# The delta rule's block inverse with full-array transposes and products in place of 64-row ones

## The reference

```
low = where(strict, einsum('bhncd,bhnsd->bhncs', k * beta, k) * decay, 0)
T = triangular_solve(eye + low, eye)          # (I + low)^-1, lower triangular
u = T @ (v * beta);  w = T @ (k * beta * exp(G))
# scan over the chunks: v_new = u - w @ s;  o = (q exp(G)) @ s + qk @ v_new;  s = s * g_last + k_dec^T @ v_new
```

## Time and profile before

| | us |
|---|---|
| median of 3 runs | 1845.88 |
| lowest and highest | 1842.76, 1850.29 |
| profiled execution, its own time | 1848.1 |
| its span, first to last instruction | 1845.4 |
| TensorE busy | 1555.1 (84%) |
| VectorE, ScalarE, GpSimd busy | 826.0, 371.3, 193.0 |
| mean granted TensorE clock | 0.90 |

### The profile page before, as it was taken

The page is one execution under the profiler, slowest core; times in us unless marked ns, Lnnn a source line. Parts: engine busy times, 40 slices in busy tenths (PEclk is TensorE's granted clock), DMA queues, the critical chain, the costliest instruction groups (busy, mean ns, idle before and its releaser), DMA issues. The chain is left out here.

```text
span 1845.4 us, 19291 instructions
## 1 busy us (share of the span) xinstructions
PE 1555.1 (84%) x7431; PEld 933.9 (51%) x7431; DVE 826.0 (45%) x1536; ACT 371.3 (20%) x702; POOL 193.0 (10%) x282
## 2 busy tenths in 40 slices
PE   4999972689999799476799859999889799999877
PEld 2877662688444444242334325444564456646563
DVE  2344549344344377442112133355664325555553
ACT  3212153111101100110001010100450134622230
POOL 0000027300000000001000000000450001202330
PEclk8899976668999899678899979999899899999887
DMA  9221002210877476669999974252300221131101
GB/s 353 79 91 46 1 1 46 53 27 4 306 244 270 175 279 219 233 254 417 416 395 365 389 263 170 91 182 69 137 1 23 91 91 46 46 136 47 47 1 46
DMA packets 126745, 283.72 MB, mean 154 GB/s; under 512 B 28568, under 2 KB 30904, under 8 KB 121403
## 3 DMA queue, kind: packets, MB, share of 16 engines
q1 hardware_dynamic: 123056, 266.78, 39.5%
q0 software_dynamic: 3600, 15.73, 2.1%
HBM read 312.90 MB, written 4.19 MB: 172 GB/s over the span
## 5 line engine op out<-in xcount | busy, mean ns | idle before, releaser
L2245 PE MATMUL ps<-hT,ring 128*128 128x512 f32 x400 | 176.4, 600 | 0.3 <-issue 0.3
L1312 PE MATMUL ps<-ring,hTx 128*128 128x512 f32 x320 | 139.2, 593 | 1.9 <-PEq L178 1.8
L2245 PEld LDWEIGHTS ps<-hT,ring 128*128 128x128 f32 x400 | 76.7, 192 | 95.7 <-issue 95.5
L2588 PE MATMUL ps<-hT,ring 128*128 128x512 f32 x256 | 113.5, 600 | 3.1 <-PEq L2495 2.7
L299 DVE SCALAR_TENSOR_TENSOR ada_acc<-ring,cact,ada_acc 128x512 f32<-128x512 f32 x154 | 104.1, 746 | 0.5
L1312 PEld LDWEIGHTS ps<-ring,hTx 128*128 128x128 f32 x320 | 60.4, 190 | 77.1 <-issue 77.1
L603 PE MATMUL ps<-hTx,ring 128*128 128x256 f32 x384 | 90.9, 392 | 5.3 <-PEq L178 5.3
L2095 PE MATMUL ps<-ring,hT 128*128 128x512 f32 x192 | 86.4, 611 | 2.6 <-PEq L178 2.4
L603 PEld LDWEIGHTS ps<-hTx,ring 128*128 128x128 f32 x384 | 74.6, 197 | 19.6 <-issue 8.0
L2588 PEld LDWEIGHTS ps<-hT,ring 128*128 128x128 f32 x256 | 48.5, 192 | 62.0 <-issue 62.0
L1845 PE MATMUL ps<-ring,hTx 128*32 128x512 f32 x384 | 52.7, 699 | 24.7 <-DMA ring<-in_expert_w 24.7
(11 more groups left out here) (519 smaller groups left out, 2589.4 us busy)
## 6 DMA issues: line engine op xcount, KB each, us to landing
ring<-in_expert_w SPq DMA_DIRECT2D x24, 2048.0 KB, 14.5
far<-in_expert_w SPq DMA_DIRECT2D x24, 2048.0 KB, 18.0
ring<-in_w_in SPq DMA_DIRECT2D x16, 2048.0 KB, 13.5
ring<-in_ada_w SPq DMA_DIRECT2D x12, 2048.0 KB, 9.3
ring<-in_w_ada SPq DMA_DIRECT2D x12, 2048.0 KB, 8.8
ring<-in_w_in_c SPq DMA_DIRECT2D x10, 2048.0 KB, 7.7
ring<-in_expert_w POOLq DMA_DIRECT2D x32, 512.0 KB
far<-in_expert_w POOLq DMA_DIRECT2D x32, 512.0 KB
```

The costliest lines, as they stand in the source:

```text
L1312: ins = pe.matmul(ps[:, 2 + i % BANKS], hTx[:, kt, t * P:(t + 1) * P], stream.slot(n)[:, kt], start=(kt == 0), stop=(kt == KT - 1))
L2245: ins = pe.matmul(bank, slot[:, kt, c0:c0 + P], hT[:, kt], start=(kt == 0), stop=(kt == KT - 1))
L2588: ins = pe.matmul(bank, slot[:, kt, j % 4 * P:(j % 4 + 1) * P], hT[:, kt], **edge)
```

## The change

The 64-row transposes become products with the whole identity's upper 64 columns: weights T (128 rows, 128 columns), moving operand `ident[:, high64]` (128 rows, 64 columns). x6 and y6 take all 128 rows and 128 weight columns too. In the half of the contraction that doesn't belong to the product one operand has to be zero: for x6 the moving `T[:, u, low64]`, and for y6 the moving `xk6`. Their other halves are cleared by GpSimd at the start of each step: the lower left part of T for both directions, and partitions 0 to 63 of `xk6`. TensorE waits for the three clears ahead of its second half. The evictions are as before.

```diff
-                        final, final_moved = ssem("final"), ssem("final_moved")
+                        final, final_moved, cleared = ssem("final"), ssem("final_moved"), ssem("cleared")
...
+                                pe.wait_ge(cleared, 3)
                                 for d in range(2):
                                     pe.wait_ge(y5_moved[d], 2)
                                     for u in range(H):
-                                        ins = pe.transpose(ps[:, 2 * d, u * 64:(u + 1) * 64], T[d][high64, u], ident[high64, high64])
+                                        ins = pe.matmul(ps[:, 2 * d, u * 64:(u + 1) * 64], T[d][:, u], ident[:, high64], start=True, stop=True)
                                     ins.then_inc(turned[d], 1)
                                     for u in range(H):
-                                        ins = pe.matmul(ps[high64, 2 * d + 1, u * 64:(u + 1) * 64], nt[low64, step, mine(d, u), high64],
-                                                        T[d][low64, u, low64], start=True, stop=True)
+                                        ins = pe.matmul(ps[:, 2 * d + 1, u * 64:(u + 1) * 64], nt[:, step, mine(d, u)], T[d][:, u, low64],
+                                                        start=True, stop=True)
                                     ins.then_inc(x6[d], 1)
                                 for d in range(2):
                                     pe.wait_ge(t_moved[d], 1)
                                     pe.wait_ge(x6_moved[d], 1)
                                     for u in range(H):
-                                        ins = pe.matmul(ps[high64, 4 + 2 * d, u * 64:(u + 1) * 64], TTr[d][high64, u, high64], xk6[high64, mine(d, u)],
+                                        ins = pe.matmul(ps[:, 4 + 2 * d, u * 64:(u + 1) * 64], TTr[d][:, u], xk6[:, mine(d, u)],
                                                         start=True, stop=True)
                                     ins.then_inc(y6[d], 1)
...
-                            if step == 0:
-                                @block.gpsimd
-                                def _(pool):
+                            @block.gpsimd
+                            def _(pool):
+                                for d in range(2):
+                                    pool.memset(T[d][high64, :, low64], 0.0).then_inc(cleared, 1)
+                                pool.memset(xk6[low64], 0.0).then_inc(cleared, 1)
+                                if step == 0:
+                                    pool.wait_ge(cleared, 3)
                                     pool.memset(t_of[1][1], 0.0)
                                     solve(pool, 1, SPLIT, BLK - 1)
```

## The result

The changed kernel takes 1891.52 us in the median of 4 runs (1885.03 to 1896.65), the kernel before 1844.88 us (1842.76 to 1850.29). The ratio is 1.0248 with a 95% interval of 1.0227 to 1.027: slower by 2.5%. The profiled execution, the slowest of the four, took 1896.65 us with a span of 1895.0 us.

What follows compares the result with a forecast made beforehand. TensorE, busy without a break at the lower clock in the inverse's second half, was taken as the bound. +11.5 us a step, +46 us over four steps, clears and tile shapes 0, gave a median of 1892 us, range 1882 to 1900.

Steps and rivals of the forecast that it cites:

- What bounds the kernel: Second half of each step's inverse: TensorE busy without a break at 0.50, so 1 us of inverse counts as 1 us.
- Instructions and their price: Second half: 96 instructions a step (80 now) at 0.213 us, 20.4 us instead of 8.92, +11.5 us a step.
- rival B: Weight loads cheaper than line 588's: 0.103 us an instruction in the second half, +4 us in all, 1850; chance 0.05.
- The clock: Second halves stay at the lower clock, 0.50, taken from line 588, whose pattern (weights set the pace) they share.
- second sum: Second half by the Trainium skill's load figure: 96 x 0.107 = 10.2 us, +1.3 us a step, 1851.
- Rival A: Clock rises before or early in each second half: sum -4 us, 1842, no measurable change; chance 0.07.
- GpSimd's clears: Three memsets a step, 2.1 us together, done before TensorE's wait: cost 0; without that cover 8 us in all.
- Rival C: Clears come late in steps 1 to 3: TensorE waits up to 2.1 us a step more, up to 1900; chance 0.05.
- Tile shapes: Dropped changes between 32x32, 64x64 and 128x128 free 0; idle time before line 1038, 0.26 us, bounds the gain.
- Phase of the clock: The scans' slow starts, 2.86 to 6.15 us, fall differently after the shift: 2 us up or down over four steps.

Runs made afterwards that it cites:

- the first experiment: Against the changed kernel: 64 weight columns instead of 128 in all three product groups, all 128 rows kept; 1826.7 us, ratio 0.9886 to the kernel before.

## Why the prediction was right

**What bounds the kernel.** Right. 46.4 us more of TensorE's work in the second halves are 46.4 us of the span, and the stages behind take the same 1379 us: nothing hid it.

**Instructions and their price.** Right: 96 a step at 0.213 us, worked out as 20.4 us, measured 20.51. That line 588's pace at 32 columns holds for 64 was the one step from a row to something the trace did not show, and the experiments confirm its reason: of rows, weight columns and moving columns up to 128, the weight columns alone set a product's pace (128 rows with 64 columns: 0.107; 128 columns with twice the moving operand: 0.213 still). So rival B is out. The figure of the Trainium skill that gave its second sum ("TensorE: Matmul & The Clock Gate", section "LDWEIGHTS (loading the stationary operand)"), 107 ns for 128 columns, is half of what a float32 product's instruction shows here at 0.50, and near the 0.113 us that it shows at 1.00. What that section of the Trainium skill says of rows, that their number does not matter to a load, agrees with the first experiment.

**The clock.** Right in outcome: 0.50 throughout all four second halves, as line 588. The reason was only half right. The prediction named two things that the new products share with line 588, a pace set by their weights and a narrow moving operand. The pace does not hold the clock down: with 128 moving columns it is the same 0.213 us, and the clock rises. Nor does the narrow operand alone: on 128 rows with 64 weight columns, at 0.107 us, the operand is as narrow, and the clock rises too. It stayed down where both came together. The transposes of the earlier trace rows that stay at 0.50 were weak evidence, for the kernel before also has 32 full-array transposes from 238.19 us on, with nothing else on TensorE, in which the clock goes up:

```profile
239.70:243.50 3.80, 3.80 (x20) 3.80 (x19) 1.38 (x2) 1.38 (x3) 0.00 (x0) 0.50 0.00 0
243.70:247.70 4.00, 4.00 (x39) 4.00 (x37) 3.24 (x5) 2.50 (x5) 0.00 (x0) 1.00 0.01 4
```

Rival A's picture was realised by other kernels. With 128 rows and 64 weight columns, or with 128 moving columns, the clock does rise, after 2.2 to 5.5 us. Its price was about right. A's sum was -4 us with the clock up from the start of the second half; with the 51.1 us that the four second halves take with the wide moving operand, instead of 4 x 10.8, it would be about +4. Measured are +1.1 +- 3 us by the ratio and +6.3 in the four steps of the profiled execution. The Trainium skill's rule of keeping TensorE busy ("TensorE: Matmul & The Clock Gate", section "Why this matters for your kernels") fails here again: 20.51 us with no break, at 0.50.

**GpSimd's clears.** Right: 0, shown by themselves. They took 2.0 us together (2.1 forecast), began 0.04 us before TensorE's first product in step 1 and ended 1.8 to 2.9 us before they were needed (1.3 us in step 1 of the kernel with the clears alone; 1 us was forecast). Rival C is out.

**Tile shapes.** Booked at 0, with 0.26 us as a bound on what dropping them could give, from the idle time before line 1038. That was the wrong place to look: the price doesn't show as idle time but in the distance of the starts, about 0.19 us at each border, inside the groups' 1.04 and 1.90 us. The second half before has three such borders a step, 0.56 us, so the bound of 0.26 was too small. The sum didn't suffer, since it replaced the whole 8.92 us; what the change gains by having one shape was in it unseen.

**Phase of the clock.** +-2 us were allowed; the scans' 20.0 us at 0.50 instead of 17.2 cost about 1.4, by the prediction's own rate of half a microsecond each.

The predicted 1892 us stand against 1891.5 measured. That they agree so closely is partly chance, since the runs themselves spread over 11.6 us. For the profiled executions the forecast was 1894.2 and the measured time 1896.65: there the time ahead of step 0's second half and step 1's first half, which the sum left as they were, took 2.3 us more.

## What to carry to other kernels

In this kernel padding a small float32 product with zeros was free in rows and costly in weight columns: fill the contraction, but load only the weight columns whose results are read. Then look at the clock: the second halves that kept all 128 rows busy at 0.107 us an instruction, or at 0.213 with 128 moving columns, went from 0.50 to 1.00, and a good part of what they won came behind them, in transposes and scans that no longer started at 0.50. Products on different halves of the rows ran side by side where they alternated and had the same tile shape; where the shapes differed, each border cost about 0.19 us at the lower clock. Turning a transpose into a 64x64 product costs a second instruction; in the alternating order it paid all the same.

## What was not expected of the hardware

- Rows seem to count for the clock. At the same pace, with the same 64 weight and 64 moving columns, products on 128 rows were at 1.00 after 2.2 to 5.5 us in each step, and the second halves with 64-row products and transposes stayed at 0.50 for 8.92 us. With two alternating 64-row tiles on different rows it rose as with one of 128.
- Doubling the moving operand of a product that is bound by its weights made the kernel 2.4% faster, 1.0006 against 1.0248.
- A change between the shapes 64x128 and 64x64 at every unit took 5.4 us a step without any idle time in the record of TensorE's products; it shows in the distance of their starts, and as gaps between the weight loads.
